# Moving the memory keys and values out of their own stage and into the mixing stage, as fp32 products

## What is computed

```python
mk, mv = memory_kv(mem_prompt, g_mem[l], w_xk[l], w_xv[l])
x = x + mixing(rmsnorm(x, g_mix), ...)        # retention, GLA and mLSTM head groups
x = x + cross_attn(rmsnorm(x, g_xattn), mk, mv, ...)
x = x + swiglu(rmsnorm(x, g_ffn), ...)
def memory_kv(mem, g_mem, w_xk, w_xv):
    mn = rmsnorm(mem, g_mem)
    k = (mn @ w_xk).reshape(B, N_MEM, X_HEADS, X_HD)
    v = (mn @ w_xv).reshape(B, N_MEM, X_HEADS, X_HD)
```

## Time and profile before

| what | us |
|---|---|
| median of 3 runs (2265.46 to 2274.37) | 2271.64 |
| the profiled execution: its own time | 2273.51 |
| its span (first to last instruction) | 2271.7 |
| PE busy, share of the span | 2035.3, 90% |
| DVE busy, share | 945.1, 42% |
| POOL busy, share | 731.4, 32% |
| ACT busy, share | 631.7, 28% |

### The profile page before, as it was taken

One profiled execution on the slowest core, in us unless ns is written; L12 is line 12 of the kernel. 1 busy time (PEld: TensorE's weight loads), 2 busy tenths in 40 slices (PEclk: granted clock), 3 DMA queues, 4 the chain that ended last, 5 costly groups with the idle time before them and its releaser, 6 DMA issues. The chain is left out here.

```text
span 2271.7 us, 32497 instructions
## 1 busy us (share of the span) xinstructions
PE 2035.3 (90%) x14188; PEld 1909.5 (84%) x14188; DVE 945.1 (42%) x1319; ACT 631.7 (28%) x867; POOL 731.4 (32%) x358
## 2 busy tenths in 40 slices
PE   6999858689899999999899996676998999999995
PEld 5899747479789999999879995574995999999994
DVE  4543677533424330232173456774234243213313
ACT  4312542023323221222151126310323332222221
POOL 3333311323123334333343332122330333333331
PEclk9999967889999999999999997777999999999997
DMA  5432101252612222222243321012534122222221
GB/s 215 148 115 85 57 0 45 86 209 75 241 39 75 83 84 93 84 83 83 99 153 132 105 75 38 1 52 105 211 140 149 65 78 83 83 93 84 84 84 51
DMA packets 61238, 219.52 MB, mean 97 GB/s; under 512 B 10612, under 2 KB 11288, under 8 KB 58792
## 3 DMA queue, kind: packets, MB, share of 16 engines
q1 hardware_dynamic: 60216, 214.32, 27.1%
q10 hardware_dynamic: 880, 3.11, 0.4%
HBM read 202.47 MB, written 11.40 MB: 94 GB/s over the span
## 5 line engine op out<-in xcount | busy, mean ns | idle before, releaser
L945 POOL TENSOR_TENSOR WL<-RAW,WH 128x1024 fp32r<-128x1024 f32 (+1 forms) x276 | 646.3, 2342 | 1206.0 <-ACT WH L984 1206.0
L544 PE MATMUL PS<-XH,WH 128*128 128x288 f32 x2880 | 623.6, 298 | 17.4 <-DVE XL L1286 12.6
L544 PE MATMUL PS<-XH,WL 128*128 128x288 f32 x2880 | 619.2, 297 | 0.0
L544 PE MATMUL PS<-XL,WH 128*128 128x288 f32 x2880 | 619.0, 297 | 0.0
L984 ACT ACTIVATE WH<-RAW 128x1024 fp32r<-128x1024 f32 x276 | 292.6, 1060 | 1099.6 <-PE PS L544 1088.3
L544 PEld LDWEIGHTS PS<-XH,WH 128*128 128x128 f32 x2880 | 467.2, 190 | 22.9 <-issue 17.7
L544 PEld LDWEIGHTS PS<-XL,WH 128*128 128x128 f32 x2880 | 466.6, 190 | 0.0
L544 PEld LDWEIGHTS PS<-XH,WL 128*128 128x128 f32 x2880 | 466.6, 190 | 0.0
L544 PE MATMUL PS<-HH,WH 128*128 128x288 f32 x704 | 151.1, 296 | 3.6 <-DVE FT L1919 3.6
L544 PE MATMUL PS<-HH,WL 128*128 128x288 f32 x704 | 150.7, 296 | 0.0
L544 PE MATMUL PS<-HL,WH 128*128 128x288 f32 x704 | 150.6, 296 | 0.0
(11 more groups left out here) (261 smaller groups left out, 2496.3 us busy)
## 6 DMA issues: line engine op xcount, KB each, us to landing
RAW<-in_w_gu SPq DMA_DIRECT2D x88, 512.0 KB, 3.2
RAW<-in_w_dn SPq DMA_DIRECT2D x48, 512.0 KB, 3.2
RAW<-in_w_in SPq DMA_DIRECT2D x44, 512.0 KB, 3.3
KV<-in_cache_k SPq DMA_DIRECT2D x32, 512.0 KB, 7.4
KV<-in_cache_v SPq DMA_DIRECT2D x32, 512.0 KB, 5.8
RAW<-in_w_xk SPq DMA_DIRECT2D x16, 512.0 KB, 4.6
RAW<-in_w_xv SPq DMA_DIRECT2D x16, 512.0 KB, 3.2
RAW<-in_w_v SPq DMA_DIRECT2D x16, 512.0 KB, 3.2
```

The source lines that it names most:

```text
L544: return nc.tensor.matmul(out, lhsT=lhsT, rhs=rhs, start=start, stop=stop)
L945: nc.gpsimd.tensor_tensor(WL[:, s, w], RAW[:, r, w], WH[:, s, w].bitcast(f32), ALU.subtract).then_inc(split_done.sem, 1)
```

## The change

The stages xk and xv are gone. The memory is normalised once a layer into MN (DVE, behind block 12 of in), in layer 0 with statistics made beside the in blocks. The keys and values become plain fp32 matmuls of MN with the unsplit weights, which lie in six slots MW: two in the space of XT, four in the space of WH and WL. There are 16 pieces a layer of the size of a unit: keys in 8 matmuls of 256 columns, values in 4 matmuls of 512. Five pieces stand ahead of the mixing loop, the other eleven in its iterations 1 to 11. PE's order there becomes `scores(i)`, `keys(i)`, the piece, `back(i - 3)`, `outputs(i - 1)`. Two PSUM banks are freed for the pieces: the outputs share a bank with the scores, so that `scores(i)` now waits for the copy of the outputs of step i - 2 (oc_ready) where it waited for the masked scores (sm_ready). ACT copies the results out. SP loads a piece when the one four places before it is used, stores every block of keys, and reloads XT after the values are stored; layer 1's tokens are written to the output y for that at the start of in.

With it go: POOL's two operations ahead of the loop (QE is cleared by ACT, KDG multiplied by DVE in two parts); the gate product moves ahead of `take_outputs`; two out units that were split before the loop are split in its iterations 12 to 14; in layer 0 SP first loads tokens and in units, and squares and splits of the tokens start with the kernel; in layer 1 they are made beside the last feed-forward blocks (dn1) of layer 0.

```diff
+MEM_UNITS, MEM_SLOTS = 16, 6
+MEM_AT = (0, 1, 2, 3, 4, 5, 2, 3, 4, 5, 2, 3, 4, 5, 2, 3)
+SCORE_BANK, KEY_BANK, LAST_BANK = (0, 6), (4, 5), (2, 3)
...
-STAGES = (("xk", 8, 8), ("xv", 8, 0), ("in", IN_BLOCKS, IN_BLOCKS), ("v", 8, 0), ("out", 8, 8),
+STAGES = (("in", IN_BLOCKS, IN_BLOCKS), ("v", 8, 0), ("out", 8, 8),
           ("xq", 8, 8), ("xo", 8, 8), ("gu0", 2 * FG, 2 * FG), ("dn0", 12, 8),
           ("gu1", 2 * FG, 2 * FG), ("dn1", 12, 8))
 U0, B0, UNITS, BLOCKS = {}, {}, 0, 0
-SHARED = 18
+SHARED = 2
...
+        MN = place("MN", [128, KB, NMEM], r_x)
+        VOUT = place("VOUT", [128, 2, D], r_x + 8192)
+        KOUT = place("KOUT", [128, 2, NMEM], r_x + 16384)
...
+        MW = [place(f"MW{i}", [128, 1024], at) for i, at in enumerate(
+            (r_x + 8192, r_x + 12288, r_wh, r_wh + 4096, r_wl, r_wl + 4096))]
...
+                if l == 0:
+                    tokens_in(0)
+                    units("in", "w_in", 0, 1)
+                    for i in range(1, 4):
+                        tokens_in(i)
+                    units("in", "w_in", 1, 3)
+                    for name, tile in (("ident", IDENT), ("ones", ONES), ("sel", SEL), ("cols", COLS)):
+                        full = tile[tuple(slice(None) for _ in tile.shape)]
+                        sp.dma_start(full, t[name]).then_inc(const_loaded.sem, 16)
+                    for name, tile in (("cmask", CMASK), ("nmask", NMASK), ("cmasks", CMASKS), ("nmasks", NMASKS),
+                                       ("rd", RD), ("qd", QD)):
+                        full = tile[tuple(slice(None) for _ in tile.shape)]
+                        sp.dma_start(full, t[name]).then_inc(masks_loaded.sem, 16)
+                else:
+                    units("in", "w_in", 0, 3)
+                    sp.wait_ge(gemm_evac.sem, gemm_evac.at(l, 0))
+                    sp.dma_start(o["y"], XT[:, :, :]).then_inc(x_spilled.sem, 16)
...
+                sp.wait_ge(unit_done.sem, unit_done.at(l, U0["v"] + 8))
+                for n in range(2, 6):
+                    memory_unit(n)
+                memory_key_out(0)
+                memory_key_out(1)
+                for n in range(6, MEM_UNITS):
+                    sp.wait_ge(mem_used.sem, mem_used.at(l, n - 3))
+                    memory_unit(n)
+                    if n < 12:
+                        memory_key_out(n - 4)
...
+                sp.wait_ge(mv_out.sem, mv_out.at(l, 2))
+                sp.dma_start(o["mem_v"][l], VOUT[:, :, :]).then_inc(vout_stored.sem, 16)
+                for stored in kout_stored:
+                    sp.wait_ge(stored.sem, stored.at(l, 64))
+                sp.wait_ge(vout_stored.sem, vout_stored.at(l, 16))
+                sp.dma_start(XT[:, :, :], t["x"] if l == 0 else o["y"]).then_inc(xt_loaded.sem, 16)
...
-                pe.wait_ge(gemm_evac.sem, gemm_evac.at(l, 0))
-                features("xk", 0, 1, MH, ML, ml_ready, 0, NMEM)
-                pe.wait_ge(msum_ready.sem, msum_ready.at(l, 1))
-                mm(bank(6, 0, NMEM), ONES[:, :], RSM[:, :], True, True).then_inc(memstat_done.sem, 1)
-                features("xk", 1, 8, MH, ML, width=NMEM)
-                pe.wait_ge(rsm_ready.sem, rsm_ready.at(l, 1))
-                for m in range(2):
-                    last = mm(bank(7, m, 1), RSM[0:1, 128 * m:128 * m + 128], ONES[0:1, 0:1], True, True)
-                last.then_inc(rtokm_done.sem, 1)
-                pe.wait_ge(gemm_evac.sem, gemm_evac.at(l, B0["xk"] + 8))
-                rows("xv", MH, ML, (0, 128), lambda ch, i: 2 * ch + i, lambda ch, i: None)
-
-
-                pe.wait_ge(xv_evac.sem, xv_evac.at(l, 2))
...
+                def memory_keys(b):
+
+                    w = memory_weights(b)
+                    if b >= 2:
+                        pe.wait_ge(mk_out.sem, mk_out.at(l, b - 1))
+                    out = bank(LAST_BANK[b % 2], 0, NMEM)
+                    for k in range(KB):
+                        last = mm(out, w[:, 128 * k:128 * k + 128], MN[:, k, :], k == 0, k == KB - 1)
+                    last.then_inc(mem_used.sem, 1)
+
+                def memory_values(n):
+
+                    w = memory_weights(8 + n)
+                    if n == 0:
+                        pe.wait_ge(mk_out.sem, mk_out.at(l, 8))
+                    elif n == 4:
+                        pe.wait_ge(mv_out.sem, mv_out.at(l, 1))
+                    for a in range(2):
+                        k = 2 * (n % 4) + a
+                        for m in range(2):
+                            last = mm(bank(LAST_BANK[m]), MN[:, k, 128 * m:128 * m + 128], w[:, 512 * a:512 * a + 512],
+                                      k == 0, k == KB - 1)
+                    last.then_inc(mem_used.sem, 1)
+
+                pe.wait_ge(mn_ready.sem, mn_ready.at(l, 1))
+                pe.wait_ge(v_evac.sem, v_evac.at(l, 8))
+                for b in range(5):
+                    memory_keys(b)
...
-                            pe.wait_ge(sm_ready.sem, sm_ready.at(l, s - 1))
+                            pe.wait_ge(oc_ready.sem, oc_ready.at(l, s - 1))
                         else:
                             pe.wait_ge(st_done.sem, st_done.at(l, s - 1))
+                    if s >= 4:
+                        pe.wait_ge(gated.sem, gated.at(l, s - 3))
...
                 for i in range(len(STEPS) + 3):
                     if i < len(STEPS):
                         scores(i)
+                        keys(i)
+                    if i == 3 * NC + 1:
+                        pe.wait_ge(mv_out.sem, mv_out.at(l, 2))
+                    if 1 <= i < 4:
+                        memory_keys(4 + i)
+                    elif 4 <= i < 12:
+                        memory_values(i - 4)
                     if 3 <= i:
                         back(i - 3, i)
-                    if i < len(STEPS):
-                        keys(i)
                     if 1 <= i <= len(STEPS):
                         outputs(i - 1)
...
-                rests("out", 0, SPLIT_SLOTS)
-                pool.wait_ge(gscan_ready.sem, gscan_ready.at(l, 1))
-                nc.gpsimd.memset(QE[:, :, :, :, :], 0.0).then_inc(qe_zero.sem, 1)
-                pool.wait_ge(gk_exp.sem, gk_exp.at(l, 1))
-                nc.gpsimd.tensor_tensor(KDG[:, :, :], KDG[:, :, :], KT[:, 3:6, :], ALU.mult).then_inc(kdg_ready.sem, 1)
...
+                def memory_key_copy(b):
+                    stored = kout_stored[b % 2]
+                    act.wait_ge(mem_used.sem, mem_used.at(l, b + 1))
+                    act.wait_ge(stored.sem, stored.at(l, 16 * (b // 2)))
+                    do(KOUT[:, b % 2, :], bank(LAST_BANK[b % 2], 0, NMEM), ACT.Copy).then_inc(mk_out.sem, 1)
+
+                def memory_value_copy(ch):
+                    act.wait_ge(mem_used.sem, mem_used.at(l, 12 + 4 * ch))
+                    for m in range(2):
+                        last = do(VOUT[:, m, 512 * ch:512 * ch + 512], bank(LAST_BANK[m]), ACT.Copy)
+                    last.then_inc(mv_out.sem, 1)
...
+                memory_key_copy(0)
                 act.wait_ge(gscan_ready.sem, gscan_ready.at(l, 1))
                 do(small("gcd", 36), small("gend", 36), ACT.Exp, scale=1.0 / 16).then_inc(act_step.sem, act_step.tick())
...
                 do(GA[:, :, :], GB[:, :, :], ACT.Exp, scale=1.0 / 16).then_inc(gexp_ready.sem, 1)
+                memory_key_copy(1)
...
+                do(QE[:, :, :, :, :].rearrange("p a q e i -> p (a q e) i"), spread(IDENT[:, :], [128, 12, CH], 1),
+                   ACT.Copy, scale=0.0).then_inc(act_step.sem, act_step.tick())
+                memory_key_copy(2)
+                memory_key_copy(3)
...
+                        if f == 1 and l + 1 < DEPTH and i in (5, 8, 11):
+                            act.wait_ge(vecs_loaded.sem, vecs_loaded.at(l + 1, 16))
+                            for k in (2 * (i // 3) - 2, 2 * (i // 3) - 1):
+                                act.wait_ge(gemm_evac.sem, gemm_evac.at(l, B0[dn] + k + 1))
+                                square(0, k, l + 1)
+                                x_upper("mix", k)
+                    if f == 1 and l + 1 < DEPTH:
+                        upper(dn, 12)
+                        for k in (KB - 2, KB - 1):
+                            act.wait_ge(gemm_evac.sem, gemm_evac.at(l, B0[dn] + k + 1))
+                            x_upper("mix", k)
+                            square(0, k, l + 1)
+                        upper(dn, 13)
...
+                if l == 0:
+                    for i in range(4):
+                        for k in (2 * i, 2 * i + 1):
+                            x_rest(0, "mix", k)
+                        if i == 0:
+                            half_rest(0)
+                        for k in (2 * i, 2 * i + 1):
+                            add_square(0, sq_ready, sq_used, 0, k)
+                    half_rest(1)
...
+                def normalise_memory():
+                    dve.wait_ge(rsm_ready.sem, 1)
+                    dve.wait_ge(mem_loaded.sem, mem_loaded.at(l, 16))
```

(16 more changed lines are left out.)

408 lines of the change are left out of this document (215 added, 193 removed).

## The result

| | before | changed |
|---|---|---|
| median of 4 runs each, us | 2273.01 (2265.46 to 2278.82) | 2190.76 (2190.56 to 2199.59) |
| span of the profiled execution | 2271.7 | 2188.8 |
| PE busy | 2035.3 | 2014.8 |
| DVE, POOL, ACT busy | 945.1, 731.4, 631.7 | 895.3, 671.5, 595.6 |

The time lies in the range of 2158 to 2226. Three of the changed kernel's four executions lie within 0.4 us of each other, the fourth is 9 us longer; the trace is of one of the three.

What follows compares the result with a forecast made beforehand. PE, 90% busy, was taken to bound the kernel outside the mixing stage, the order within a step inside it. Savings of 123.9 us less 29.2 for both layers' mixing gave -94.7 on 2273.5: 2179 us, range 2158 to 2226.

Steps and rivals of the forecast that it cites:

- What goes: Memory stages ahead of in: 66.0 us saved at layer 1's border, 57.9 in layer 0's start, 123.9 together.
- What the transfers need: Layer 1's token store and XT's reload are covered, about 1.5 us to spare at block 3; counted at nothing.
- Ahead of the loop: Five key pieces fit PE's 23.13 us idle stretch, DVE's KG product gets shorter; loop starts 3.2 us earlier a layer.
- What a piece costs: Each key or value piece takes PE 3.45 us at 2.4 GHz, 6.9 at 1.2.
- In the loop: Mixing loop walked step by step with a piece per iteration: 113.1 us against 95.31, +17.8 a layer.
- the forecast's own case: The forecast total of 2179 from 2160 (loop of 106, start 3 better) to 2198 (loop of 121); chance 0.65.
- What else moves: Memory statistics, ACT's squares, clearing and copies, POOL's missing work, late out units, key stores: all counted at nothing.
- rival 1: In the loop the clock falls as before, mean 0.80: 38 us more a layer, 2225 or so; chance 0.18.
- rival 2: The whole loop stays at 1.2 GHz: +128 us a layer, 2405, slower than before; chance 0.03.
- Rival 3: The pieces lie in idle time entirely, the loop stays at 95 us: 2143; chance 0.04.
- Rival 4: Late weights, a piece waiting for its slot, or a load-paced layer 0 start: 5 to 25 us, 2185 to 2205; 0.10.
- Rival 5: Layer 1's in blocks still wait for memory work of DVE or ACT; chance under 0.01.

Runs made afterwards that it cites:

- e6: Changed kernel with layer 0's loads in the old order, constants, masks and memory ahead of tokens and in units; 2199.88 us (one run).
- e5: Changed kernel storing 8 KB instead of the 2304 KB of tokens at layer 1's start, reload from the input in both layers; 2192.69 us (one run).
- e4: Changed kernel with the product KDG x KT back on POOL as one instruction and none on DVE; 2200.88 us (one run).
- e1: Changed kernel with ACT copying the first half of the values out in iteration 7 instead of 8; 2181.97 us, ratio 0.9595.
- e2: Changed kernel with the eleven loop pieces cut to one matmul of 256 columns each, loads, copies, waits and order kept; 2136.48 us (one run).
- e3: Changed kernel with each loop piece at the head of its iteration and its ACT copy ahead of that iteration's other work; 2152.01 us, ratio 0.9456.
- e11: Changed kernel with the piece at the head of the iteration in GLA steps alone, copies on ACT early; 2161.81 us (one run).
- e9: e3 with the fifth key copy behind the first QE copies on ACT and ACT's table loaded before the tokens land; 2149.61 us, ratio 0.9454.

## Why the prediction was right, and where it was off

**What goes** held to a microsecond at both places: -58.7 for -57.9 in layer 0, -66.2 for -66.0 in layer 1, with no gap at the border. e6 shows the first as a chain from the loads on; it was not DVE alone that set its pace.

**What the transfers need** held. The cover of 1.5 us was 0.7, and e5 shows that nothing of it reaches PE.

**Ahead of the loop** held: -4.3 and -2.9 us for -3.2 each. e4 shows the part of POOL's product in it, about 2 us a layer. The PE wait of 1.64 for QE behind the fifth key copy was not in the sum and lay inside its 1.5.

**What a piece costs** held: 3.45 us from its first matmul to the next instruction, keys and values alike, wherever the clock was full.

**In the loop** is the step that failed, by 7.2 and 8.7 us. Its walk was right to 0.9 us (112.2 for 113.1), with a retention step of 9.2 for 8.7, GLA 10.3 for 10.7, mLSTM 9.4 for 9.7. That the sum is so close is in part luck, since these three misses cancel. The loops of 120.3 and 121.9 stand at the upper edge of the forecast's own case (121), and the total is nearer than they are because the other stretches came out 4 us cheaper. Two terms were missing in the walk:
- 3.84 us a layer for the copy of the values. It had no term: under "What else moves" I looked at the key stores, two steps ahead of the next copy, and not at the one bank hand-over without a step between. The question to ask was which ACT instruction stands ahead of the copy: the exponential of KG, late itself. e1 shows it gone.
- 4.3 and 5.9 us a layer for spells at the lower clock. "Full clock in the loop" was the assumption I named as the largest; the mean is 0.96 and 0.95 instead of 1, far from the 0.80 of rival 1, and what lies between had no case of its own.

**The reason for the clock** that I gave was half right at most: "at most one or two waits, with a dense piece between". e2 with hardly any pieces holds 0.91 and has 2.9 us in all its KG groups, so it isn't the dense piece as such that lifts the clock from 0.80. Nor is it the sum of the waits, which is 18.4 us in e2's loop and 12.4 in the one before. What is left of the reason is the row of three stops in one step (a retention step, where the prediction says mLSTM), which is gone; no run tests it by itself, so the cause of the rise from 0.80 to 0.91 stays open. Of the rest up to full clock the runs show more: e3, where the pieces stand ahead of every wait but the two of iteration 12 and end them, holds 1.00. The Trainium skill says in "TensorE: Matmul & The Clock Gate", A second HAM failure mode: psum-queue depth-cycling, that short idles between groups of matmuls make the clock swing; with that these traces agree: the spells take 4.9 and 8.3 us in e1 with all waits, 1.6 and 1.6 in e11 with the longer ones covered, and nothing in e3, where all but two are. What the rule doesn't give is when a spell comes, and the runs leave that open too: the same 1.12 us wait starts one in one GLA step and none in the next, and e2 has more idle time than the loop before at a higher clock.

**The rivals.** Rival 1 (the swing of before, 2225) and rival 2 (1.2 GHz throughout, 2405) are refuted by the granted clock. Rival 3 (the pieces in idle time entirely, 2143) is refuted for this kernel, where they cost 27 us of 33; but e3 and e9 come to 2152 and 2150, near it, for a reason that I had not seen: not because PE had enough idle time before, but because a piece at the head of the step stands exactly in the time of the waits. Rival 4 had the right kind of thing, a piece that waits, but for a slot of weights and not for a bank. Rival 5 falls by the trace: in matmuls follow dn1 without a gap.
